# All projections first: modulation units and two groups of output gates moved behind them in the mixing stage of a hybrid decoder step

## Time and profile before

| | |
|---|---|
| median of three runs | 1295.23 us |
| profiled execution | 1295.95 us, span 1294.2 us, mean PE clock granted 0.937 |
| PE busy | 1181.3 us, 91% of the span |
| DVE / ACT busy | 576.7 (45%) / 387.1 (30%) |
| first mix matmul to last chain matmul | 62.1 to 475.0 us |
| first product of the gate stage | 480.6 us |
| first merge-gate product (P8) | 538.9 us |
| last lift to first output product | 791.2 to 793.1 us |

### The profile page before, as it was taken

The page is one execution under the profiler, slowest core; times in us unless marked ns, Lnnn a source line. Parts: engine busy times, 40 slices in busy tenths (PEclk is TensorE's granted clock), DMA queues, the critical chain, the costliest instruction groups (busy, mean ns, idle before and its releaser), DMA issues. The chain is left out here.

```text
span 1294.2 us, 26861 instructions
## 1 busy us (share of the span) xinstructions
PE 1181.3 (91%) x11789; PEld 1103.0 (85%) x11789; DVE 576.7 (45%) x1048; ACT 387.1 (30%) x531; POOL 11.9 (1%) x29
## 2 busy tenths in 40 slices
PE   5679879989977779999999999969999999989997
PEld 3478868878866659999999998959999999989996
DVE  1355966567777563433333335462222222353322
ACT  1343482372221005722222221142222322331121
POOL 0000110000000000000000000000000000000000
PEclk9779989989996659999999999979999999989998
DMA  9802643123260016525333221312332332223201
GB/s 304 255 3 91 137 153 100 55 86 114 80 162 7 2 35 66 150 66 153 90 90 90 89 82 33 98 33 68 95 97 68 94 97 60 74 78 90 72 20 70
DMA packets 191033, 116.76 MB, mean 90 GB/s; under 512 B 36650, under 2 KB 189351, under 8 KB 190678
## 3 DMA queue, kind: packets, MB, share of 16 engines
q1 hardware_dynamic: 190358, 115.16, 32.0%
q0 software_dynamic: 576, 0.14, 0.1%
HBM read 108.31 MB, written 6.96 MB: 89 GB/s over the span
## 5 line engine op out<-in xcount | busy, mean ns | idle before, releaser
L813 PE MATMUL ps<-high_parts,scr_parts 128*128 128x272 f32 x2976 | 577.0, 293 | 16.8 <-DVE hT_parts L2703 8.2
L813 PEld LDWEIGHTS ps<-high_parts,scr_parts 128*128 128x128 f32 x2976 | 474.2, 190 | 22.3 <-issue 8.7
L813 PE MATMUL ps<-hT_parts,scr_parts 128*128 128x272 f32 x1552 | 431.9, 290 | 0.0
L2600 DVE TENSOR_TENSOR scr_parts<-ring,scr_parts 128x1024 fp32r<-128x1024 f32 (+1 forms) x108 | 138.6, 1284 | 338.6 <-ACT scr_parts L1780 335.7
L1780 ACT ACTIVATE scr_parts<-ring 128x1024 fp32r<-128x1024 f32 (+1 forms) x108 | 119.6, 1108 | 566.2 <-PE ps L813 539.9
L813 PEld LDWEIGHTS ps<-hT_parts,scr_parts 128*128 128x128 f32 x1552 | 288.9, 190 | 0.0
L813 PE MATMUL ps<-pj_parts,scr_parts 128*128 128x272 f32 x992 | 168.8, 295 | 5.7 <-DVEq L1910 5.7
L813 PEld LDWEIGHTS ps<-pj_parts,scr_parts 128*128 128x128 f32 x992 | 142.8, 191 | 7.3 <-DVEq L1910 6.4
L813 PE MATMUL ps<-high_parts,pj_parts 128*128 128x272 f32 x352 | 110.7, 315 | 24.9 <-ACT rstd L1651 7.9
L813 PE MATMUL ps<-high_parts,ring_parts 128*128 128x272 f32 x352 | 105.1, 299 | 0.0
L813 PE MATMUL ps<-hT_parts,pj_parts 128*128 128x272 f32 x352 | 105.0, 298 | 0.0
(11 more groups left out here) (323 smaller groups left out, 1079.4 us busy)
## 6 DMA issues: line engine op xcount, KB each, us to landing
ring<-in_w_in_dram SPq DMA_DIRECT2D x62, 512.0 KB, 5.4
ring<-in_ada_w_dram SPq DMA_DIRECT2D x48, 512.0 KB, 5.1
ring<-in_ffn_w_in_dram SPq DMA_DIRECT2D x44, 512.0 KB, 5.0
ring<-in_ffn_w_out_dram SPq DMA_DIRECT2D x16, 384.0 KB, 3.6
ring<-in_ffn_w_out_dram SPq DMA_DIRECT2D x16, 320.0 KB, 4.1
ring<-in_w_out_dram SPq DMA_DIRECT2D x8, 512.0 KB, 4.0
x_scratch<-scr SPq DMA_DIRECT2D x1, 2176.0 KB, 13.1
scr<-x_scratch SPq DMA_DIRECT2D x1, 2176.0 KB, 11.4
```

Source lines behind the costliest of these rows:

```text
L813: return pe.matmul(out, lhsT, rhs, start=start, stop=stop, skip_group_check=True)
L2600: dve.tensor_tensor(lo, src, hi.bitcast(F32), SUB).then_inc(w_split, 1)
```

## The change

- `SEQUENCE` has 22 mix units (`EARLY`) first, then the 8 pairs of ada and turn, then 4 more mix units: the output gates of SSD (`SZ`) and mLSTM (`MO`). In the planner a unit behind the first 22 goes only where no chain stage could start in the meantime (`FILL`), and the last four wait for the end of the SSD chain (`s_statec`) and the read of ada unit 6.
- `Z_ORDER` keeps two groups, so the gate stage has 4 output-gate products (P0 to P3) and the merge gates are P4 to P35. `LAG` becomes 8, which keeps the lifts behind P12 and following; eight lifts are left at the end instead of four.
- ACT reads the SZ unit out of PSUM only when the 8 stores of the SSD sample states are done, since they lie in the same tile. Silu of SZ is taken ahead of the gate-stage loop. `o_rs2` and `o_rs3` now stand behind the sigmoid of merge gates 0 and 1.
- The mLSTM sample state is loaded into other tiles, once the SSD chain has ended. Some scratch is laid out anew: `wx_hi` is a buffer of its own, `g_ub` shares a tile with `gAt` and is cleared once per pair of chunks.
- The first two merge-gate loads wait for the late mix units (their slots) instead of for splits; they stay where they are in SP's order, behind all state stores.

```diff
-Z_ORDER = [8, 3, 7, 14]
+EARLY = 2 * len(MIX_ORDER)
+MIX_ORDER += [8, 14]
+Z_ORDER = [3, 7]
-LAG = 4
+LAG = 8
-for _n in range(2 * len(MIX_ORDER)):
-    SEQUENCE.append(("mix", _n))
-    if _n >= 8 and _n % 2 == 1:
-        SEQUENCE.append(("ada", _n // 2 - 4))
-    if _n >= 10 and _n % 2 == 0:
-        SEQUENCE.append(("turn", _n // 2 - 5))
-SEQUENCE += [("turn", 6), ("ada", 7), ("turn", 7)]
+SEQUENCE += [("mix", _n) for _n in range(EARLY)]
+for _n in range(8):
+    SEQUENCE += [("ada", _n), ("turn", _n)]
+SEQUENCE += [("mix", _n) for _n in range(EARLY, 2 * len(MIX_ORDER))]
...
+            behind = kind == "mix" and v >= EARLY
+            filler = unit >= EARLY
+            known = all(n in when for n in needs) and not (behind and late is None)
+            start = max([free["pe"]] + [when.get(n, 0.0) for n in needs] + ([late + 4.0] if behind and late else []))
+            if filler and known:
+                for c in chains:
+                    if at[c] < len(chains[c]):
...
+                        if begin < start + FILL:
+                            known = False
...
-            loads = window + [("z", n) for n in range(R)]
+            loads = window + [("z", n) for n in range(counts["z"])]
...
-            sp.wait_ge(x_done, TILE_DONE[-1])
+            rest.after(sp, NT, "s_statec")
             for p in range(2):
                 for q in range(2):
                     sp.dma_start(Q_c[q * DK:(q + 1) * DK, p], A["state_mlstm_c"][0, :, 2 * p + q].rearrange("b k v -> k b v")).then_inc(d_q["mlstm"], 16)
...
-            rest.after(sp, NT, "s_statec")
...
             for idx in range(counts["gate"]):
-                sp.wait_ge(w_split, 2 * idx + 2)
+                if idx < 2:
+                    sp.wait_ge(x_done, TILE_DONE[EARLY + 2 * idx + 1])
+                else:
+                    sp.wait_ge(w_split, 2 * idx - 2)
                 load("gate", slot_of("gate", idx), idx)
...
+                    if f == SZ:
+
+                        act.wait_ge(q_out["ssd"], 128)
                     act.activation(pj[:, f, h * HN:(h + 1) * HN], ps[:, h, 0:HN], ACT.Copy).then_inc(x_read, 1)
...
-            for m in range(2):
-                high(m + 2)
-                z_out(m, ACT.Silu)
-            for m in range(2, M_GATE):
+            for z in (SZ, SZ + 1):
+                act.activation(pj[:, z, :], pj[:, z, :], ACT.Silu).then_inc(z_ready, 1)
+            for m in range(M_GATE + 2):
                 n = m - 2
                 high(m + 2)
-                z_out(m, ACT.Copy)
-                if n < 4:
+                if m < M_GATE:
+                    z_out(m)
+                else:
+                    gate_out(m - M_GATE)
+                if n >= 0:
                     mid.begin(act, 0, f"o_rs{n}")
...
-            for k in range(4 * KD):
+            for k in range(2, 4 * KD):
...
-                    if t == 0:
-
-                        dve.memset(g_ub[0][DK:P, :], 0.0)
-                        dve.memset(g_ub[1][0:DK, :], 0.0)
...
+                        if n == lv[-1]:
+
+                            dve.memset(g_ub[0][DK:P, :], 0.0)
+                            dve.memset(g_ub[1][0:DK, :], 0.0)
```

More of the change, by code:

```diff
@@ L26 @@
 T = 512
-B0, C0, SCR = 5632, 9216, 12672
+B0, C0, SCR = 5120, 8704, 11264
 NB, ND = 8, 4
@@ L242 @@
 WEIGHT = 0.003
+FILL, LOADED = 0.7, 9.0
 COST = {"pe": 1.2, "dve": 1.2, "act": 0.9}
@@ L305, in shared_order @@
                 best = (start, "x", evac[0][1], "read", "act")
-        if split < len(mix_tiles):
+        late, freed = when.get(("s", NT, "s_statec")), when.get(("x", ADA_READ[6]))
+        late = max(late, freed + LOADED) if late is not None and freed is not None else None
+        if split < (EARLY if late is None else len(mix_tiles)):
             e, side = stage_ // 2, stage_ % 2
@@ L310, in shared_order @@
                 eng = "dve" if side else "act"
-                start = max(free[eng], when[need])
+                start = max(free[eng], when[need], late if split >= EARLY else 0.0)
                 if best is None or start <= best[0]:
@@ L321, in shared_order @@
                 needs.append(("lo", v, part_ // 2))
-            known = all(n in when for n in needs)
-            start = max([free["pe"]] + [when.get(n, 0.0) for n in needs])
+            behind = kind == "mix" and v >= EARLY
[5 more added lines that the diff above has]
+                    if at[c] < len(chains[c]):
+                        t, name, eng = chains[c][at[c]]
+                        begin = max(free[eng], ready[c]) + (0.0 if eng == "pe" else cost(name, eng, t) + 0.1)
+                        if begin < start + FILL:
+                            known = False
             if known and (best is None or start < best[0]):
@@ L421, in trunk @@
         Q_s, Q_g, Q_h, Q_c = (pj[:, f:f + 2, :].rearrange("k a n -> k (a n)")[:, 0:1024].rearrange("k (p b v) -> k p b v", p=2, b=NB)
-                              for f in Z_TILES[::2])
-        wx_hi = pj_parts[:, Z_TILES[-2]:Z_TILES[-1] + 1, :].rearrange("p a n -> p (a n)")[:, 0:1024].rearrange("p (e c) -> p e c", e=2)
+                              for f in (SZ, GZ, HG, SB))
+        wx_hi = ctx.enter_context(nc.sbuf_tensor("wx_hi", [P, 2, 512], F32R))
         vrow = part(4488, 2 * P).rearrange("p (a c) -> p a c", a=2)
@@ L430, in trunk @@
         gT, gU, gX, gL, gD, gAt, g_vb, g_kn, g_kd, g_qs = (part(512 * n, 512) for n in range(10))
-        g_u, g_u1 = part(5120, 256), part(5376, 256)
+        g_u, g_u1 = gAt[:, 0:256], gAt[:, 256:512]
         g_kb, g_w, g_sk = gX, gX, gT
@@ L441, in trunk @@
         s_acc, s_spad, s_tail, s_hist = part(B0, 1088), part(B0 + 1088, 224), part(B0 + 1312, 512), part(B0 + 2720, 512)
[L443 to L446, removed]
+        hD, hQ, hQK, hEf = (part(C0 + 512 * n, 512) for n in range(4))
+        hKdV = part(C0 + 1024, 1024)
+        S_h1, S_h2, S_h3 = (part(C0 + 2048 + P * n, P).rearrange("k (p v) -> k p v", p=2) for n in range(3))
+        hKdV_s = part(C0 + 2048, 512)
+        hKd, hV = hKdV_s[:, 0:256], hKdV_s[:, 256:512]
         h_Ue = part(C0, 2048)
@@ L1786, in _, with z_out @@
             high(1)
-            def z_out(m, func):
+            def z_out(m):
                 act.wait_ge(w_done, m + 1)
-                act.wait_ge(*((q_out["ssd"], 128), (q_out["gdn"], 64), (q_out["hgrn"], 64), (q_out["mlstm"], 64))[m // 2])
-                act.activation(two(pj[:, Z_TILES[m], :]), ps[:, 2 * (m % 2):2 * (m % 2) + 2, 0:HN], func).then_inc(gate_read, 1)
+                act.wait_ge(q_out[("gdn", "hgrn")[m // 2]], 64)
+                act.activation(two(pj[:, Z_TILES[m], :]), ps[:, 2 * (m % 2):2 * (m % 2) + 2, 0:HN], ACT.Copy).then_inc(gate_read, 1)
             def gate_out(k):
@@ L1825, in _ @@
                 act.activation(pj[:, z, :], pj[:, z, :], ACT.Sigmoid).then_inc(z_ready, 1)
-            for k in range(4 * KD):
+            for k in range(2, 4 * KD):
+                if k == GBUF.index(SB):
+                    act.wait_ge(q_out["mlstm"], 64)
                 if k == len(GBUF):
@@ L1834, in _ @@
                     merged_high((k - LAG) // 4 - 1)
+            for d in range((4 * KD - 4 - LAG) // 4, 6):
+                merged_high(d)
             act.wait_ge(lin_done, 4 * KD - 3)
@@ L2256, in gdn_dve @@
                         dve.tensor_tensor(gU, gU, ps[:, 5, :], SUB)
-                        if n != lv[-1]:
+                        if n == lv[-1]:
+                            dve.memset(g_ub[0][DK:P, :], 0.0)
+                            dve.memset(g_ub[1][0:DK, :], 0.0)
+                        else:
                             dve.tensor_tensor(gT, gT, ps[:, 4, :], SUB)
@@ L2408, in hgrn_dve @@
                     else:
-                        dve.tensor_copy(hKdV[0:m, 0:512], ps[0:m, 6, :])
+                        dve.tensor_copy(hKdV_s[0:m, :], ps[0:m, 6, :])
                     done(hgrn)
@@ L2607, in _ @@
                 if n == 2:
-                    dve.wait_ge(gate_read, 2)
+                    dve.wait_ge(z_ready, 2)
                 for f in range(2):
@@ L2627, in _ @@
                 if n != 2:
-                    dve.wait_ge(z_ready, (2, 4, 4, 6)[n])
+                    dve.wait_ge(z_ready, (4, 6, 2, 8)[n])
                     for f in range(2):
```

## The result

The changed kernel takes 1281.78 us (median of four runs, 1279.81 to 1282.67) where the kernel before takes 1296.18 (1294.41 to 1298.27): a ratio of 0.9887, 95% interval 0.9873 to 0.9902, so 14.4 us less. The forecast was 1281.

The account below looks back on a forecast made before the run. The mixing stage was taken as bound by PE until 341 us, then by chains on a half-fed PE. Terms -15.7 + 22.6 + 2.0 - 24.2 + 0.6 = -14.7 against 1295.95 gave 1281 us, range 1265 to 1295.

Parts of the forecast that it names:

- The mLSTM chain starts some 28 us earlier: Mixing stage: modulation units leave from between the mix units, so mix unit 21 ends about 27.7 us earlier.
- The last chain matmul at 459: End of the mixing stage: five terms sum to 15.7 us earlier, from 475.0 to about 459.
- Idle time I gave 7.9 + 12.4: Mixing stage: 7.9 us idle behind modulation units goes, and half of 24.7 us idle behind unit 21 is filled.
- the clock I gave 9.5: Mixing stage behind unit 21: wide products raise the granted clock, winning a third of up to 29.5 us.
- Two units exposed, P0 at H + 15.4, with a clock that is up: Start of gate stage: mix units 24 and 25 add 12.1 us behind the chains, then reads and P0 without slow start.
- H: The time at which the last chain matmul ends: 475.0 us before, about 459 forecast.
- The gate load lands at H + 46.8 and PE waits: Ahead of P4: merge gate 0's weights land late, PE waits 12.5 us, plus 2.0 for the clock afterwards.
- The Silu passes hold P8 by 2.7: Gate stage on ACT: Silu and Sigmoid passes right behind the last Exp make P8 wait 2.7 us.
- From P8 on -23.6: Rest of the gate stage: four fewer products give -24.2 us, four more lifts standing alone cost +0.6.
- the load was not in time: Judges the rival that gate loads arrive in time and P4 does not wait: 14.5 less, 1267 us; chance 0.16.
- the clock in the sample stages stayed low: Judges the rival that wide products keep the clock up through sample stages: 10 us more gained, 1271; chance 0.14.
- the slower rival: Mixing stage: units put ahead of ready chain matmuls hold the mLSTM chain; H rises by 6, 1303 us; chance 0.10.

Follow-up runs that it names:

- modulation_only: Kernel before, only unit order changed: 22 mix units first, then ada and turn pairs in gaps, all output gates kept in the gate stage; 1274.91 us.
- gate_loads_first: Changed kernel with the first two merge-gate loads ahead of the mLSTM state stores in SP's order; 1268.92 us, 0.9791 of the kernel before.
- silu_later: Changed kernel with the Silu and Sigmoid passes over the output gates two rounds later on ACT; 1276.47 us, 0.9852 of the kernel before.
- both_waits_out: Changed kernel with the first two merge-gate loads ahead of the ten small stores and the Silu and Sigmoid passes two rounds later; 1266.11 us.

## Why the prediction was right

- *The mLSTM chain starts some 28 us earlier*: it starts 32.2 us earlier (311.29 against 343.49). Mix unit 21 ends not 27.7 but 38.9 us earlier (302.0 against 340.9); up to there, from 156 us on, PE idles 9.7 us against 15.4 and the granted clock is 0.98 against 0.94, and the term had only 7.9 of idle in it. The SSD chain, not a projection, is now what the mLSTM chain waits for. `modulation_only` shows that this move alone brings the last chain matmul forward.
- *The last chain matmul at 459*: 458.0. Here two terms were mis-sized and offset each other. Idle time I gave 7.9 + 12.4 = 20.3, and it gave 14.4; the clock I gave 9.5, and it gave 14.7. That the sum came within 1.3 us is in part luck. The SZ read's wait, put at 2, was 3.8 us of ACT ("ACT pj L1666 <- DMA out_dram<-pj: 3.8" in the waits).
- *Two units exposed, P0 at H + 15.4, with a clock that is up*: H + 14.9, but the step on the clock failed. P0 to P2 took 19.8 us (472.94 to 492.73) where three products of 6.05 are 18.2, so I had counted 1.6 us as saved that were not: behind the 2.69 us in which PE waited for `low(0)` the granted clock was 0.72 for 6 us.
- *The gate load lands at H + 46.8 and PE waits*: `high(4)` at H + 45.3, ended by the DMA. The wait was 7.80 us and not 12.5, for three reasons of about equal size: the load landed 1.5 us earlier against H, P0's slow start had eaten 1.6 of the wait, and the squares between Ln and the sums were mis-sized. From `high(4)` to the sums it takes 5.7 us and not 7.1, as two squares and not four stand there. Behind the wait, sums and P4 take 10.4 us (508.95 to 519.38) instead of 7.9, so the clock cost 2.5, where I had 2.0 (taken from P0's slow start before, which I had put to 5.55 us of idle; but PE had run at a granted 0.50 ahead of that idle too, from 458 to 475 us). From the sums ahead of P3 to those ahead of P5 it is 26.7 us against 15.8 in `gate_loads_first`: 10.9 in all, where I had 14.5.
- *The Silu passes hold P8 by 2.7*: 3.43 seen, and 5.2 with the clock behind it by `silu_later`; I had no term for that clock. The table loads show no drain: the load at 536.34 starts 0.13 us behind the pass before it and takes 1.28, and the Silu pass starts at 537.63. The Trainium skill (ScalarE: Activation LUTs, "What ACT_TABLE_LOAD costs") puts a drain of about 1380 ns on top of each switch, by which my estimate of the wait was 13.7; the trace disagrees, and decides.
- *From P8 on -23.6*: -22.4. The term that failed is not the lifts: the four more that stand alone add 7.3 us (16.9 against 9.6 from the row of lifts to the first output product), 1.8 each, what a lift takes between products too. The 1.8 us that are missing are P8's slow start, at a granted 0.72 behind the 3.43 us of idle. From there to the lifts PE has no gap in either kernel.
- *The rivals*: the load was not in time; the clock in the sample stages stayed low (0.67 from 423 to 458 us, 0.58 from 423 to 475 before), and the clock's 14.7 is half of the 29.5 that I had as its most; the chains were not held as the slower rival has it, and without the gap rule they end some 9 to 13 us later.

The mechanisms hold: the earlier start of the mLSTM chain, the two exposed units, the late load and the passes ahead of P8 are all in the profile, and four experiments show three of them one by one: the start of the chain, the load, and the passes. That the total came within 1 us of the forecast is in part luck: up to the last chain matmul two misses of 5 to 6 us offset each other, and in the gate stage a wait put 3.6 us too long, with the clock behind it, offsets the slow starts of P0 and P8 (1.6 and 1.8) that I had not counted.

## What to carry to other kernels

When work is moved out of a stage, look at what it covered: the four products gone from the gate stage had been hiding a weight load behind 25 us of stores, and two plain rounds of ACT. A DMA that a later stage needs belongs well ahead of the small strided stores in its queue: here they delayed its landing by some 11 us and its issue by 6. Test the parts of a change by themselves: here one part alone was worth 20.5 us by the medians (19 by the ratio) and the whole 14.4, and with the two waits taken out it is 30.4. A wait of PE costs more than its length where the granted clock is low behind it: the 3.43 us ahead of P8 were worth 5.2.

## What was not expected of the hardware

- Ten stores of 4-byte-wide states delay a 512 KB load issued behind them to 15.6 to 17.0 us. Issued ahead of them it lands in 4.2 to 6.6, but the one issued last, 1.7 us ahead of the first of the stores, took 15.6.
- Behind the same 2.69 us of idle PE ahead of P0, five profiles have a granted clock of 0.71 or 0.72 in the 6 us that follow and lose 1.6 us on P0 to P2; `both_waits_out` has 1.00 and loses nothing. In all six PE had run at 1.00 just before. Why the one differs is open:

```profile
479.60:485.60 6.00, 6.00 (x47) 6.00 (x48) 1.08 (x1) 2.14 (x3) 0.00 (x0) 1.00 0.77 181
```

- From 440 to 450 us PE is busy all 10 us at a granted 0.50 in `modulation_only` as before the change: first matmuls of 4 columns, then from 445.73 the state updates of 512 columns on 32 rows. In this stretch PE has no gap and still half the clock.
